# Between the halves of a transformer block: the second weight's low half in two parts, h handed on block by block, and products of ones in TensorE's gaps

## The reference

```
def sublayer(x, sidx, fn, res_w):
    shift = mod[:, sidx, 0][:, None, :]
    scl = mod[:, sidx, 1][:, None, :]
    gate = mod[:, sidx, 2][:, None, :]
    hh = rms_norm(x, norm_g[i, 2 * sidx]) * (1.0 + scl) + shift
    return x + res_w * gate * rms_norm(fn(hh), norm_g[i, 2 * sidx + 1])

x = sublayer(x, 0, lambda hh: swiglu(hh, ffn_w1[i, 0], ffn_w2[i, 0]), 0.5)
...
x = sublayer(x, 1, mixer, 1.0)
x = sublayer(x, 2, lambda hh: swiglu(hh, ffn_w1[i, 1], ffn_w2[i, 1]), 0.5)
```

## Time and profile before

| | us |
|---|---|
| median of 3 runs | 3505.67 |
| lowest, highest | 3503.44, 3506.58 |
| the profiled execution, its own time | 3508.46 |
| span of the profile (first to last instruction) | 3506.2 |
| TensorE busy | 2979.7 |
| DVE busy | 2494.3 |
| ACT busy | 1334.5 |
| mean granted clock of TensorE, of 1 | 0.919 |

### The profile page before, as it was taken

The page is one execution under the profiler, slowest core; times in us unless marked ns, Lnnn a source line. Parts: engine busy times, 40 slices in busy tenths (PEclk is TensorE's granted clock), DMA queues, the critical chain, the costliest instruction groups (busy, mean ns, idle before and its releaser), DMA issues. The chain is left out here.

```text
span 3506.2 us, 48085 instructions
## 1 busy us (share of the span) xinstructions
PE 2979.7 (85%) x18803; PEld 2385.0 (68%) x18803; DVE 2494.3 (71%) x4398; ACT 1334.5 (38%) x2189; POOL 504.0 (14%) x307
## 2 busy tenths in 40 slices
PE   7976865566655599988999998999998999999899
PEld 4856752222211188878888887888887888888787
DVE  3677748888889788676869726887834886567665
ACT  1041111111111154465444446444445544445643
POOL 1020025445555300000000050000031000000000
PEclk9998877877777799999999999999998999999999
DMA  8933229999999977524849641867742774543153
GB/s 346 384 126 122 99 90 368 387 391 394 391 410 407 402 301 266 190 82 166 352 173 370 240 146 49 363 230 314 279 184 78 297 279 174 185 182 139 72 193 120
DMA packets 122951, 853.91 MB, mean 244 GB/s; under 512 B 17412, under 2 KB 18436, under 8 KB 20868
## 3 DMA queue, kind: packets, MB, share of 16 engines
q1 hardware_dynamic: 85604, 582.56, 43.1%
q0 software_dynamic: 36864, 268.45, 18.7%
q10 hardware_dynamic: 288, 0.26, 0.0%
HBM read 850.11 MB, written 1.11 MB: 243 GB/s over the span
## 5 line engine op out<-in xcount | busy, mean ns | idle before, releaser
L204 DVE TENSOR_TENSOR w_lo<-w_ring,w_hi 128x2048 fp32r<-128x2048 f32 x304 | 695.0, 2288 | 328.6 <-ACT w_hi L199 328.5
L674 PE MATMUL ps<-h_pair,w_hi 128*128 128x512 f32 x2560 | 889.8, 397 | 2.6 <-PEq L1021 1.3
L199 ACT ACTIVATE w_hi<-w_ring 128x2048 fp32r<-128x2048 f32 x330 | 630.4, 1913 | 399.2 <-PE ps L288 290.8
L678 PE MATMUL ps<-h_pair,w_lo 128*128 128x256 f32 x2560 | 665.6, 281 | 0.0
L674 PEld LDWEIGHTS ps<-h_pair,w_hi 128*128 128x128 f32 x2560 | 464.3, 188 | 93.1 <-issue 4.0
L678 PEld LDWEIGHTS ps<-h_pair,w_lo 128*128 128x128 f32 x2560 | 483.0, 189 | 29.1
L3174 PE MATMUL ps<-expert_rows,expert_diag 128*128 128x512 f32 x412 | 292.0, 850 | 225.7 <-ACT expert_diag L3215 225.7
L272 DVE CUSTOM_DVE_ANT_0 a_ring<-a_ring,cond_row 128x1024 f32<-128x1024 f32 x288 | 340.9, 1236 | 64.5 <-DMA a_ring<-in_t_stream 61.9
L3174 PEld LDWEIGHTS ps<-expert_rows,expert_diag 128*128 128x128 f32 x412 | 93.9, 251 | 417.2 <-ACT expert_diag L3215 338.3
L204 POOL TENSOR_TENSOR w_lo<-w_ring,w_hi 128x2048 fp32r<-128x2048 f32 x26 | 120.3, 4641 | 1540.3 <-ACT w_hi L199 1540.3
L3134 POOL DMA_INDIRECT expert_rows<-in_experts,expert_idx x206 | 281.2, 1365 | 321.5 <-DVE expert_sum L3327 150.5
(11 more groups left out here) (473 smaller groups left out, 4955.5 us busy)
## 6 DMA issues: line engine op xcount, KB each, us to landing
w_ring<-in_w_stream SPq DMA_DIRECT2D x376, 1024.0 KB, 4.9
a_ring<-in_a_stream SPq DMA_DIRECT2D x108, 1024.0 KB, 7.4
a_ring<-in_t_stream SPq DMA_DIRECT2D x36, 1024.0 KB, 10.0
a_ring<-in_m_stream SPq DMA_DIRECT2D x8, 1024.0 KB, 7.6
alibi<-in_alibi SPq DMA_DIRECT2D x3, 2048.0 KB, 8.1
cond_row<-in_cond_row SPq DMA_DIRECT2D x8, 512.0 KB, 3.7
expert_rows<-in_experts,expert_idx POOLq DMA_INDIRECT x206, 11.8
gates<-mod_rows SPq DMA_DIRECT2D x3, 1024.0 KB, 5.7
```

The costliest lines, as they stand in the source:

```text
L199: act.activation(self.w_halves(n)[0], self.w_item(n), ACT.Copy).then_inc(self.hi_made, 1)
L204: pool.tensor_tensor(self.w_halves(n)[1], self.w_item(n), self.w_halves(n)[0], ALU.subtract).then_inc(self.lo_made, 1)
L674: both = lambda: pe.matmul(core.ps[:, bank, :], w_hi[:, k, cols], core.h_pair[:, :, k, :], start=k == 0, stop=k == KD - 1)
L678: pe.matmul(core.ps[:, bank, 0:T], w_lo[:, k, cols], core.h_split[0][:, k, :], start=False, stop=False)
```

## The change

It has four parts, all in `Tail`.

1. In ffn_stage's tail the low half of the second weight (2048 columns) is made in two instructions of 1024: blocks 0 to 3 on DVE before tile 1's reciprocal (a new wait there for the high half), blocks 4 to 7 after the first four blocks of h. TensorE waits for the first part by a semaphore of its own (`lead_half_made`) and for the second by `lo_made` at block 4.
2. `H_PARTS`: h is handed on in parts of 1, 1, 2, 2 and 2 blocks, where it was 2, 2, 2 and 2, in all twelve tails.
3. Between the transposes of tile 0 and of tile 1 TensorE does 6 products of ones of 512 columns in ffn_stage's tail and 2 in the others, into bank 3.
4. Behind the transposes of tile 1 it does 2 more, in all.

```diff
+H_PARTS = [(0, 1), (1, 2)] + [(k, k + 2) for k in range(2, KD, 2)]
...
@@ modulate
-            if k % 2:
+            if k == 0 or k % 2:
                 last.then_inc(self.whole_made.sem, 1)
...
@@ vector_apart
             if self.pre is not None:
+                if t == TT - 1:
+                    n = core.w_taken + LEAD - 1
+                    dve.wait_ge(core.hi_made, n - core.split_from + 1)
+                    self.split_lead(dve, 0).then_inc(self.lead_half.sem, 1)
                 self.scale_rows(dve, t, 2 * t + 2)
         if self.pre is not None:
-            core.split_lo(dve, core.w_taken + LEAD - 1)
-            self.split_h(dve)
+            self.split_h(dve, apart=True)
+
+    def split_lead(self, dve, half):
+        core, n = self.core, self.core.w_taken + LEAD - 1
+        ks = slice(half * KD // 2, (half + 1) * KD // 2)
+        hi, lo = (w[:, ks, :] for w in core.w_halves(n))
+        return dve.tensor_tensor(lo, core.w_item(n)[:, ks, :], hi, ALU.subtract)
 
-    def split_h(self, dve):
+    def split_h(self, dve, apart=False):
         core, done = self.core, self.core.dve_steps.done
-        for k in range(0, KD, 2):
-            dve.wait_ge(self.whole_made.sem, self.whole_made.at(k // 2 + 1))
-            hi, lo = (part[:, k:k + 2, :] for part in core.h_split)
-            done(dve, dve.tensor_copy(hi, self.whole[:, k:k + 2, :]))
-            dve.tensor_tensor(lo, self.whole[:, k:k + 2, :], hi, ALU.subtract).then_inc(self.h_made.sem, 1)
+        for i, (k, to) in enumerate(H_PARTS):
+            dve.wait_ge(self.whole_made.sem, self.whole_made.at(i + 1))
+            hi, lo = (part[:, k:to, :] for part in core.h_split)
+            done(dve, dve.tensor_copy(hi, self.whole[:, k:to, :]))
+            dve.tensor_tensor(lo, self.whole[:, k:to, :], hi, ALU.subtract).then_inc(self.h_made.sem, 1)
+            if apart and to == KD // 2:
+                self.split_lead(dve, 1).then_inc(core.lo_made, 1)
         core.split_lo(dve, core.w_taken + LEAD)
...
@@ tensor
         for t in range(TT):
+            if t:
+                core.keep_busy(pe, 6 if apart else 2, 3, slice(0, BANK))
             for k in range(KD):
...
+        core.keep_busy(pe, 2, 3, slice(0, BANK))
         first = core.w_taken
+        starts = [k for k, _ in H_PARTS]
         for k in range(KD):
-            if k % 2 == 0:
-                pe.wait_ge(self.h_made.sem, self.h_made.at(k // 2 + 1))
+            if k in starts:
+                pe.wait_ge(self.h_made.sem, self.h_made.at(starts.index(k) + 1))
             for u in range(LEAD):
-                if k == 0:
+                if apart and u == LEAD - 1:
+                    if k == 0:
+                        pe.wait_ge(self.lead_half.sem, self.lead_half.at(1))
+                    elif k == KD // 2:
+                        core.split_wait(pe, first + u)
+                elif k == 0:
                     core.split_wait(pe, first + u)
```

More of the change, by code:

```diff
@@ L327, in __init__ @@
         names = ("y_ready", "yg_made", "squares_ready", "x_new", "xn_made", "turned_ready", "h_whole_made",
-                 "roots_ready", "h_split_made")
+                 "roots_ready", "h_split_made", "lead_half_made")
         (self.y_ready, self.yg_made, self.squares, self.x_new, self.xn_made, self.turned,
-         self.whole_made, self.roots, self.h_made) = [core.semaphore_of(n) for n in names]
+         self.whole_made, self.roots, self.h_made, self.lead_half) = [core.semaphore_of(n) for n in names]
         self.n_post = 2 * TT if post is not None else 0
@@ L486, in warm, with tensor @@
                       start=True, stop=True)
-    def tensor(self, pe, warm=WARM):
+    def tensor(self, pe, warm=WARM, apart=False):
         core = self.core
@@ L520, in tensor, with passed @@
                     last.then_inc(core.w_used, 1)
-    def passed(self):
+    def passed(self, apart=False):
         n_pre = TT if self.pre is not None else 0
@@ L529, in passed @@
         self.xn_made.passed(2 * n_pre)
-        for x in (self.turned, self.whole_made, self.h_made):
-            x.passed(KD // 2 if n_pre else 0)
+        self.turned.passed(KD // 2 if n_pre else 0)
+        for x in (self.whole_made, self.h_made):
+            x.passed(len(H_PARTS) if n_pre else 0)
+        self.lead_half.passed(1 if n_pre and apart else 0)
 def pre_stage(core, pre):
@@ L734, in _ @@
             pe.sem_inc(w_used, 1)
-            tail.tensor(pe, WARM // 2)
+            tail.tensor(pe, WARM // 2, apart=True)
         @block.scalar
@@ L870, in ffn_stage @@
     hidden.passed(FF_STEPS)
-    tail.passed()
+    tail.passed(apart=True)
     core.split_issued = splits.stop
```

## The result

The change takes 3477.86 us (median of 4 runs, 3469.83 to 3483.01) where the kernel before takes 3504.69 us (3503.44 to 3506.58) beside it: a ratio of 0.9919, 95% interval 0.9907 to 0.9932, so 26.8 us less. Forecast were 3471 us in a range of 3460 to 3481. The two profiled executions are 3508.46 and 3479.70 us, 28.8 us apart, with spans of 3506.2 and 3477.5 us.

A forecast was written before the change was run, and what follows sets the result against it. TensorE, 85% busy, was taken as the bound, waiting for h and slowed by its clock. Terms 12.5 + 16.6 + 3.4 + 0.85 + 1.5 = 34.9 us gave 3473.6, forecast as 3471 us; 8-in-10 range 3460 to 3481.

The forecast's parts named there:

- Low half, first part: Ffn passages: half the subtraction moves into DVE's idle time before tile 1's reciprocal, takes 1.22 us and costs nothing.
- First block alone: Ffn passages: h's first block, cast and subtracted alone, lets TensorE start 1.78 us earlier; seven times, 12.5 us.
- Later blocks: Ffn passages: DVE delivers h's later blocks before TensorE wants them; three more DVE instructions per passage stay hidden.
- The clock, 16.6 us: Seven ffn passages: with short gaps the clock stays at 1.00 over h's products, saving 16.6 us; bounds 0 and 16.6.
- four output passages: Passages after output projections: gaps of 0.7, 0.48 and 1.65 us left the clock up, taken as evidence for ffn passages.
- The sum and the median: Whole kernel: the terms sum to 34.9 us, 3473.6 by the profiled execution; the runs' median lies 2.8 us lower, so 3471.
- What I can't price well: Stages behind the first passage: shifted timing may add or remove a clock fall, as in compression, 6.4 us either way.
- likeliest case: Whole kernel: the forecast outcome around 3471 us, with its own range 3462 to 3478; chance 0.82.
- The clock still falls: Rival, ffn passages: the clock drops anyway, only earlier starts remain, 16.8 us, giving 3489 us; chance 0.09.
- A better alignment: Rival, layer 0 and the like: clock falls there vanish too, 3464 us or less; counted within the forecast's 0.82.
- Slower: Rival, ffn passages: the second weight's high half is late and delays tile 1, +14.6 us, 3520 us; chance 0.02.
- Doesn't do what it says: Rival, stages behind the passages: bound elsewhere, they return the time; within 7 us of before; chance 0.01.

The follow-up runs named there:

- e3: The change with ACT's high half of the second weight moved behind tile 1's square and root: 3505.32 us, ratio 0.9982.
- e5: The change with h handed on in pairs again (2, 2, 2, 2): 3483.40 us, ratio 0.9932.
- e7: The change with the second weight's low half whole again, between row scaling and the split of h: 3484.46 us, ratio 0.9931.
- e4: The kernel before, unchanged, profiled once more: 3509.07 us.
- e1: The change without its products of ones in both places: 3478.93 us, ratio 0.9917.
- e9: The change, with TensorE starting h's first block on its high half and doing low-half products last: 3462.69 us, ratio 0.9873.
- e6: The change with one 512-column product of ones before every fourth compression product in layers 0 and 3: 3479.88 us, ratio 0.9916.

## Why the prediction was right

**Low half, first part.** Right: 1.22 us forecast and measured, in DVE's idle time, the reciprocal not moved. e3 shows that a late high half would have cost its whole lateness.

**First block alone.** Right: cast 0.29 and subtraction 0.43 us as assumed, start of h 1.88 us behind the start of tile 1's transposes, 1.78 earlier in seven passages and 0.86 in five. e5 puts the block's part at 0.85 us in each of twelve, e7 the low half's move at 1.38 in each of seven. (They overlap: either alone leaves the other as the next wait, 0.93 and 0.40 us earlier than before.)

**Later blocks.** Right: TensorE waits for DVE nowhere behind the first block; 11.50 us of products. DVE's busy time in such a window rose from 5.2 to 7.0 us and stayed hidden. The Trainium skill's advice on tiles of at least 512 elements (VectorE: DVE Perf Modes, the TRN2 errata) names a fixed cost for each instruction. The trace agrees: subtractions of 256 and 1024 columns took 0.43 and 1.22 us, which leaves about 0.16 us that doesn't shrink with the size. It cost nothing here because DVE is not what ends last in these windows.

**The clock, 16.6 us.** The size was right, the reason only in part. The prediction put it down to the products of ones; the runs show 10.0 us with the earlier start alone, 9.3 with the ones alone, 16.6 with both. That the four output passages never fall was read from one execution; e4 has one that fell. So the size came out as the best case (7 x 11.50 us) on evidence that didn't carry it, and in that the forecast had luck. On transposes that do not count as busy (the Trainium skill, TensorE: Matmul & The Clock Gate, PE-mode transpose) the trace leaves it open: in e7 the clock held over transposes, ones and 1.73 us of idle time, in e1 it fell in 4 of 7 and held in 3 of 7 with transposes and no ones.

**The sum and the median.** 34.9 us in the passages, forecast and measured. The median moved by 26.8. The forecast of 3471 was 7 us low, and the step to name is "What I can't price well": falls in the attention layers were taken as symmetric around the one profile at hand, and so put at nothing in the sum. That profile, like the second one, has 624.9 us there; the three of the change have 626.6 to 633.8. About 2 us of this are the stick layer's and came with the change each time. Whether the change makes the other falls likelier or met them by chance, five profiles can't say. The range, made wide by just this, held the result, which lies at the upper end of the likeliest case (3462 to 3478).

**The rivals.** "The clock still falls" did not happen with the change in any of 21 ffn passages of three profiles. "A better alignment" did not come: the attention layers took longer. "Slower" did not come either: the reciprocal did not move. "Doesn't do what it says" is out: the ffn stretches behind the passages are 176.6 us before and after, and of 34.9 us the attention layers took back 7.9 in the first profile.

## What to carry to other kernels

Where a busy engine waits a short while at a seam, ask first which instruction stands between the data and it that could stand elsewhere: a weight's half moved into an idle 1.5 us, and the first block handed on alone, gave 1.78 us a seam, and e9 gave 0.46 more by starting with the products that need only what is ready. What held TensorE's clock at these seams was no single piece (the earlier start alone 10.0 us, the ones alone 9.3, both 16.6), so price such pieces together and not one by one. And where the clock falls by chance in other stages, a median of four runs carries several us that are not the edit's: read an edit's worth from its own place in the trace.

## What the runs showed of the hardware that was not expected

- TensorE's granted clock fell to 0.50 while the engine counted as busy: the 128x60 products of the compression take 7.33 us for 64 at 1.00 and 11.51 us with the fall. A window inside the latter, kernel before:

```profile
1503.00:1506.00 3.00, 3.00 (x16) 3.00 (x15) 2.86 (x11) 0.00 (x0) 0.00 (x0) 0.50 0.27 82
```

- With one product of 512 columns before every four of them (e6) the clock was at 1.00 in both stages of the one profile, at 3.2 us a stage.
- At the same place in the same program the clock falls in one execution and not in the next: 25.9 and 19.5 us.
- The transposes themselves run slower at the lower clock: eight take 1.97 us in e3 where they took 1.09.
